# A decoder step with 576 expert gathers: the state space part by groups of four tokens, block 0 finished before the other blocks' projections and attention

## The reference, cut to what matters

```
[q | k | v | u] = x @ w_in + b_in                    # four parts of 512 columns
att = mixture of dilated causal windows over q, k, v  # 8 heads of 64
ssm = S5 state space over u: 32 groups of 16 channels, 64 complex states each
      h[t] = a * h[t-1] + B u[t];  y[t] = Re(C h[t]) + D u[t];  then gelu, a GLU
h   = LN1(ALPHA * x + concat(rms(att), rms(ssm)) @ w_out + b_out)
y   = LN2(ALPHA * h + PEER(h) + sigmoid(h @ w_ple_gate) * (p @ w_ple))
# PEER: 8 heads; h @ w_pq gives queries (4 parts of 512 columns), matched with 128 + 128
# keys; the 16 best of their pairs name experts, each a row of w_down and a row of w_up:
#     sum over experts of  weight * gelu(h . down[e]) * up[e]
```

## Time and profile before

| what | value |
|---|---|
| median of 3 runs | 1949.74 us (1948.12 to 1951.41) |
| profiled execution: its own time, its span | 1951.28 us, 1949.5 us |
| mean granted clock of TensorE | 0.741 of full |
| busy share: PE, DVE, ACT, POOL | 68%, 69%, 41%, 40% |
| moved by the DMA engines | 723.17 MB, of which the gathers 604.02 MB |
| chain that ended last: DMA, PE, DVE, ACT, issue | 37%, 22%, 13%, 7%, 6% |

### The profile page before, as it was taken

The page is one execution under the profiler, slowest core; times in us unless marked ns, Lnnn a source line. Parts: engine busy times, 40 slices in busy tenths (PEclk is TensorE's granted clock), DMA queues, the critical chain, the costliest instruction groups (busy, mean ns, idle before and its releaser), DMA issues.

```text
span 1949.5 us, 23865 instructions
## 1 busy us (share of the span) xinstructions
PE 1326.9 (68%) x7204; PEld 646.9 (33%) x7204; DVE 1350.4 (69%) x3212; ACT 793.6 (41%) x2757; POOL 777.9 (40%) x796
## 2 busy tenths in 40 slices
PE   7999886774764866656664655555746666677876
PEld 6765572331232333324321222122221333322221
DVE  6967898864748779888987753444444467886665
ACT  2132247772424344544543443333333223354554
POOL 0953324443434444455443333233233344444442
PEclk9999996776886677777776677766767555576977
DMA  7012689999999999999999999999999999999997
GB/s 299 1 44 93 200 312 421 397 373 421 411 387 415 352 421 421 421 421 420 417 391 416 421 414 420 420 421 421 422 412 422 421 420 405 412 416 417 413 422 287
DMA packets 101024, 723.17 MB, mean 371 GB/s; under 512 B 12016, under 2 KB 12784, under 8 KB 20784
## 3 DMA queue, kind: packets, MB, share of 16 engines
q0 software_dynamic: 82944, 604.02, 75.5%
q1 hardware_dynamic: 17968, 117.77, 15.4%
HBM read 714.78 MB, written 4.87 MB: 369 GB/s over the span
## 4 chain that ended last, share of the span: by engine, by line
DMA 37%; PE 22%; DVE 13%; ACT 7%; issue 6%; POOL 1%; POOLq 0%; ACTq 0%; DVEq 0%; another core or an unknown queue 0%
DMA R<-d_uv,W 37%; PE bank L1408 8%; DVE R L2169 7%; PE bank L1321 3%; PE bank L1295 3%; PE bank L1162 3%; ACT W L1682 1%; ACT L1679 1%; PE bank L1291 1%; PE bank L1154 1%; ACT W L1687 1%; PE bank L1355 1%; POOL R L919 1%; PE bank L1208 1%; ACT W L1650 1%
## 5 line engine op out<-in xcount | busy, mean ns | idle before, releaser
L919 POOL DMA_INDIRECT R<-d_uv,W x576 | 671.8, 1166 | 1011.1 <-PE bank L1408 832.0
L2169 DVE CUSTOM_DVE_ANT_0 R<-R,W 128x1024 f32<-128x1024 f32 x576 | 696.7, 1223 | 473.1 <-DMA R<-d_uv,W 456.1
L1408 PE MATMUL bank<-R,W 128*32 128x512 f32 x2296 | 473.4, 848 | 558.9 <-ACT W L1687 550.5
L1650 ACT CAST W<-W 128x2 uint32<-128x2 f32 x292 | 55.7, 192 | 883.5 <-DVE W L2169 866.8
L1408 PEld LDWEIGHTS bank<-R,W 128*32 128x32 f32 x2296 | 81.6, 125 | 798.5 <-ACT W L1687 724.6
L1687 ACT ACTIVATE W<-W 128x32 f32<-128x32 f32 x576 | 153.5, 313 | 9.7
L1682 ACT ACTIVATE W<-W 128x1 f32<-128x1 f32 x576 | 138.2, 287 | 9.7
L1321 PEld LDWEIGHTS bank<-E 128*128 128x128 f32 x864 | 123.7, 230 | 35.7 <-issue 35.7
L1321 PE MATMUL bank<-E 128*128 128x128 f32 (+1 forms) x864 | 129.7, 317 | 0.5 <-issue 0.5
L963 PE MATMUL bank<-E,W 128*128 128x256 f32 (+1 forms) x384 | 102.9, 427 | 10.1 <-DMA E<-d_xT 7.9
L963 PEld LDWEIGHTS bank<-E,W 128*128 128x128 f32 x384 | 75.4, 200 | 31.5 <-issue 10.1
(11 more groups left out here) (334 smaller groups left out, 1807.9 us busy)
## 6 DMA issues: line engine op xcount, KB each, us to landing
E<-d_kc SPq DMA_DIRECT2D x8, 2560.0 KB
E<-d_w_pq SPq DMA_DIRECT2D x6, 2048.0 KB, 12.7
E<-d_vc SPq DMA_DIRECT2D x8, 1536.0 KB, 26.2
R<-d_uv,W POOLq DMA_INDIRECT x576
E<-d_w_out SPq DMA_DIRECT2D x4, 2048.0 KB, 12.7
E<-d_vc SPq DMA_DIRECT2D x8, 1024.0 KB, 30.5
W<-d_w_in SPq DMA_DIRECT2D x3, 2048.0 KB, 21.1
W<-d_w_pq SPq DMA_DIRECT2D x3, 2048.0 KB, 8.2
```

The lines of the kernel that those rows point to most:

```text
L919: pool.indirect_dma_start(ring[r], None, A["uv"], bass.IndirectOffsetOnAxis(ap=stage[:, half, s:s + 1], axis=0),).then_inc(landed[r], 16)
L1408: last = mm(acc(half, TG * column_group(js[s], half), TG), wsel[:, r, :], ring[r][:, D + half * 512:D + half * 512 + 512], start=False, st ...
L1650: return nc.scalar.copy(stage[:, half, PAIR * x:PAIR * x + PAIR], egall[:, 0, at])
L2169: last = nc.vector.tensor_tensor_reduce(ring[r][:, 0:D], ring[r][:, 0:D], hrep[:, js[s], :], 1.0, 0.0, ALU.mult, ALU.add, dots[:, x, s:s + 1])
```

## The change

**State space part.** The 512 tokens are taken as 128 chunks of four (`SUB`, `CHUNKS`), and x is laid out with the tokens of a block ordered by their place in the chunk. Inside a chunk the convolution is done by one matrix of 128 x 128 for each group of 32 channels (`T`), which is made on the chip; between chunks runs the scan, with the fourth power of the decay. So one scan holds the whole prompt: `scan` is run 4 times and not 16, POOL carries nothing between blocks, and it runs the sample's recurrence behind the fourth scan.

- `piece_u`: u for 128 channels is 128 products of 32 columns that write 32 rows each, by place in the chunk, into one bank of 512; four such pieces and one for the sample (`us`).
- `turn_b`: 32 transposes that lay out B times the powers of the decay, made by DVE (L1333 to L1346 of the changed kernel); `make_c` (DVE): C times the powers, 31 operations; `kernel_of`, four times 48 products with 4 copies each: the matrix `T`.
- `ssm_in` four times, 8 products over all 128 rows; `ssm_out` four times, 12 products; `z_turn` four times, 16 products and a copy, which put the tokens in order for the GLU after gelu.

**Order.** Ahead of block 0's attention come only the halves of k and q that hold blocks 0 and 1 (x = 0) and v of block 0. q's other halves stand between the heads. k's other halves come behind the first match, and the part of `w_in` that they need is loaded a second time (`w_again`, 2 MB). v of blocks 2, 3 and 4 comes at pairs 0 to 2, the GLU of blocks 1 to 3 at pairs 1 to 7, and of block 0's asks the second behind the first pick, the third at pair 8, the fourth at pair 14. POOL is given four slots after the first projection, two after k's last piece and two after the second ask. The attention of blocks 1 to 3 begins at pair 4 with the spacing as before, `PROJECT_AT` is 38, and picks 1, 2 and 3 are at pairs 1 to 10, 17 to 26 and 25 to 38. The bias table of the attention is loaded in three parts, for block 0 (`pbias_first`), for block 1 (`pbias_second`) and whole.

```diff
...
+    order += [("free", 1), ("ask", 0, 1, 0), ("ask", 0, 1, 1), ("free", 2), ("ask_out", 0, 1), ("match", 0, 1), ("match_out", 0, 1)]
...
-ATT_AT = 1
-GLU_AT = 7
-PROJECT_AT = 35
+ATT_AT = 4
+PROJECT_AT = 38
...
+    for b, glu in ((1, 1), (2, 3), (3, 5)):
+        at[glu].append(("glu_block", b))
+        at[glu + 1].append(("gate_block", b))
+        at[glu + 2].append(("product_rest", b))
+        at[8].append(("sums_rest", b))
...
+    for b, t in ((2, 0), (3, 1), (4, 2)):
+        at[t].append(("piece", number("v", b, 0)))
...
+    look_rest(8, 2)
+    look_rest(14, 3)
...
-    pick(1, 0, 0, 0, 0, 0, 1, 2, 3, 4, 5)
-    pick(2, *range(6, 22, 2), 22, 23)
-    pick(3, *range(24, 40, 2), 40, 41)
+    pick(1, 1, 2, 3, 4, 5, 6, 7, 8, 9, 10)
+    pick(2, *range(17, 27))
+    pick(3, 25, 27, 29, 31, 32, 33, 34, 35, 37, 38)
...
+                for j in range(4):
+                    for k in range(DC):
+                        for step in range(SUB):
+                            o = bank[32 * step:32 * step + 32, c, j * P:j * P + P].rearrange("p (a b) -> p a b", a=QB)
+                            last = mm(o, w_u(c)[:, k, 32 * j:32 * j + 32], xT_by_step[:, :, k, step, :],
+                                      start=(k == 0), stop=(k == DC - 1), skip_group_check=True)
...
+            def kernel_of(q):
...
+                for j in range(4):
+                    for x in range(2):
+                        for step in range(SUB):
+                            r = slice(32 * step, 32 * step + 32)
+                            mm(bank[r, 4, j * P:j * P + 32 * (SUB - step)], Bs[:, 4 * q + j, x, :],
+                               C[:, 4 * q + j, x, 0:SUB - step, :].rearrange("p a b -> p (a b)"),
+                               start=(x == 0), stop=False, skip_group_check=True)
...
+            def free(n):
+
+                if n == 0:
+                    pe.wait_ge(out_full, 1)
+                    pe.wait_ge(at_squared, 1)
+                elif n == 1:
+                    pe.wait_ge(proj_full, number("k", CT - 1, 1) + 1)
+                else:
+                    pe.wait_ge(pq_full, 2)
+                pe.sem_inc(slot_free, HALF if n == 0 else PAIR)
...
```

More of the change, by code:

```diff
@@ L52 @@
 FIRST_BANKS = 1024
-WIDE = [2 * P, 2 * P + ST]
+SUB = 4
+CHUNKS = SEQ // SUB
 ROUND = 1.5 * 2.0 ** 23
@@ L135, with number, piece_bank @@
+def number(kind, c, x):
+    return PIECES.index((kind, c, x))
+def piece_bank(n):
+    kind, c, x = PIECES[n]
+    if kind in ("k", "q") and x == 0 or kind == "u":
+        return c
+    if kind == "us":
+        return 4
+    if kind == "v" and c < 2:
+        return 3
+    return 6 + n % 2
 UNITS = [(qb, h) for qb in range(QB) for h in range(NH)]
 def order_of_front():
-    steps = 4 * QB
-    pieces = {n: [2 * CT + 2 * n, 2 * CT + 2 * n + 1] for n in range(9)}
-    pieces.update({n: [2 * CT + 9 + n] for n in range(9, 12)})
@@ L210, in order_of_front, with unit, turned, piece @@
-    order += [("ask", 0, 3, 0), ("ask", 0, 3, 1), ("free", 2, 3),
-              ("ask_out", 0, 3), ("match", 0, 2), ("match_out", 0, 2), ("match", 0, 3), ("match_out", 0, 3)]
+    def unit(k, *whats):
+        return [(what, i) for what in whats for i in (2 * k, 2 * k + 1)]
+    def turned(k):
+        return unit(k, "turn_probs", "invert") + [("copy_pt", 2 * k + 1)]
+    def piece(kind, c, x):
+        n = number(kind, c, x)
+        return [("piece", n), ("put_v" if kind == "v" else "put", n)]
@@ new lines, in order_of_front @@
+    order = [x for c in range(3) for x in piece("u", c, 0)] + [("turn_b", g) for g in range(8)]
+    order += [("tm", 0), ("ssm_in", 0)] + piece("us", 0, 0) + [("s_in",)] + piece("u", 3, 0)
+    order += [("scan", 0), ("ssm_in", 1), ("tm", 1), ("make_c",)]
+    order += [x for c in range(3) for x in piece("k", c, 0)]
+    order += [("kernel_of", 0), ("ssm_out", 0), ("scan", 1), ("ssm_in", 2), ("tm", 2), ("kernel_of", 1)] + piece("k", 3, 0)
+    order += [("gelu", 0), ("ssm_out", 1), ("kernel_of", 2), ("kernel_of", 3), ("scan", 2), ("ssm_in", 3), ("tm", 3)]
@@ new lines, in order_of_front @@
+    order += piece("q", 0, 0) + [("z_turn", 0), ("gelu", 1), ("ssm_out", 2)] + piece("q", 1, 0) + [("z_turn", 1), ("gelu", 2)]
+    order += piece("q", 2, 0) + piece("q", 3, 0) + [("z_turn", 2), ("piece", number("v", 0, 0))]
+    order += [("scan", 3), ("put_v", number("v", 0, 0)), ("ssm_out", 3)] + unit(0, "scores", "bias", "exps")
+    order += [("gelu", 3)] + turned(0) + unit(1, "scores", "bias", "exps")
+    order += piece("q", 0, 1) + [("z_turn", 3)] + turned(1) + unit(0, "values") + unit(2, "scores", "bias", "exps")
@@ new lines, in order_of_front @@
+    order += [("project_first", n) for n in (3, 2, 0, 1)] + [("rms_inverse", 0), ("residual", 0), ("root", 0)]
+    order += [("normal", 0, 0), ("normal", 0, 1), ("turn", 0), ("turn_out", 0), ("ask", 0, 0, 0), ("ask", 0, 0, 1)]
+    order += [("ask_out", 0, 0), ("match", 0, 0), ("match_out", 0, 0), ("s_ssm_out",), ("free", 0)]
+    order += [("tops", 0, 0, j) for j in range(4)] + piece("k", 0, 1) + piece("k", 1, 1)
+    order += [("cross", 0, 0, 0), ("cross", 0, 0, 1), ("resolve", 0, 0, 0), ("resolve", 0, 0, 1)] + piece("k", 2, 1)
@@ L725, in _ @@
+            rows(0)
+            sp.wait_ge(at_full, 1)
+            sp.wait_ge(at_squared, 1)
+            load(parts_of[0][0], eight(A["w_pq"][0]), in_pq[0])
             sp.wait_ge(sx_ready, 1)
@@ new lines, in z_turn @@
+            def z_turn(q):
+                pe.wait_ge(y_used, q + 1)
+                if q == 0:
+                    pe.wait_ge(t_ready, CT)
+                else:
+                    pe.wait_ge(z_ready, q)
+                for step in range(SUB):
+                    for j in range(4):
+                        last = mm(bank[32 * j:32 * j + 32, 4, step * P:step * P + P],
+                                  ident[:, 32 * step:32 * step + 32], zt[:, j, :], start=True, stop=True)
+                last.then_inc(z_turned, 1)
@@ L1714, in finish_root @@
                 f(lnrow[:, 2:3], lnrow[:, 1:2], ACT.Sqrt).then_inc(y_root, 1)
-            parts = {"piece": put, "tm": set_tm, "s_in": copy_ssm_in, "exps": exps, "norm_out": norm_out,
+            parts = {"put": put, "z_turn": z_turn, "turn_b": put_b, "kernel_of": put_t, "tm": set_tm, "s_in": copy_ssm_in, "exps": exps, "norm_out": norm_out,
                      "copy_pt": copy_pt, "squares": squares, "att_out": att_out, "gelu": gelu,
```

888 lines of the change are left out of this document (495 added, 393 removed).

## The result

| | before | changed |
|---|---|---|
| median, us | 1950.58 (1948.12 to 1952.72, 4 runs) | 1983.76 (1974.8 to 1989.98, 4 runs) |
| ratio, 95% interval | | 1.0167 (1.0126 to 1.0208) |
| profiled execution's span | 1949.5 | 1973.0 |

What follows compares the result with a forecast made beforehand. PE bounds the front, the DMA engines everything from the first gather on. Span 1949.5 - 17.6 (earlier gather) + 26.9 (moved bytes) = 1958.8, median 1959 us, 0.5% slower; range 1937 to 1976.

Steps and rivals of the forecast that it cites:

- (a): PE's work up to the first projection's end: end at 206.6 us, 14.0 earlier; with (b), first gather 17.6 us earlier.
- the price of 67 ns: Cost of each narrow product of u on PE, giving 8.6 us a piece and 34.6 us for four.
- The price of a stall in the clock: In the front, PE slowed by a lower clock behind a wait: 3.0 us more, taken twice, 6.
- The rival of slow narrow products: u's products in the front cost 0.1 us each, 17 us longer, 1976; chance 0.14, shared with "the cover is gone".
- (b): From the first projection's end to the first gather: 7.1 us to h, then 36.9, gather at 250.6.
- A rule and a row: Front: DVE's scans priced alone, up to 60 us longer beside POOL; attention beside POOL's sample work 10 us by the lock.
- (c): Loads and stores moved behind the first gather: 11.3 MB, adding 26.9 us at 421 GB/s.
- (d): PE's added work between the pairs (v, GLUs, two asks): bounds 0 and 8 us, taken as 0.
- The sign named for (d): PE's wait for the fourth ask's w_pq at pair 14, and DVE's for the bias table, show whether (d) is 0.
- The other sign: If DVE's picks are late for block 0's second expert group, POOL waits for W and not for slots.
- The faster rivals: Moved bytes fill gaps behind the first gather, or the front is much shorter: each 1942 us; together, faster, 0.20.
- the cover is gone: Between the pairs, (d)'s 8 us, plus lower clocks at six waits (12 us): 1979; chance 0.14, shared with slow narrow products.

Runs made afterwards that it cites:

- a_again: The changed kernel measured once more with no edit: 1988.94 us, ratio 1.0197 to the kernel before.
- c_light: a_both with v of blocks 2 to 4 and the third and fourth ask summed over one of eight parts: 1959.55 us, ratio 1.0042 to before.
- c_bytes: c_light with only the still used eighth of w_pq loaded for the two asks, 3.67 MB less: 1958.01 us, ratio 1.0040 to before.
- a_both: Changed kernel with block 2's second residual moved ahead of block 1's transposition, and GLU sums and asks spread over pairs: 1972.30 us, ratio 1.0113 to before.
- a_picks: a_both with DVE's picks 2 and 3 laid wider, at pairs 14 to 26 and 28 to 41: 1977.37 us, ratio 1.0141 to before.

## Why the prediction was wrong, point by point

- **(a) The front, 17.6 us earlier: right, a little small.** It is 22.3. PE, timeline of the changed kernel (answers to the earlier trace rows): the pieces of u, `turn_b`, and the fourth piece.

```profile
...
10.49 8.60 PE L971 MATMUL bank<-E,W 128*32 128x128 f32 x223 [10.49 <-DMA E<-d_xT]
...
33.16 8.39 PE L971 MATMUL bank<-E,W 128*32 128x128 f32 x289 [2.77 <-issue]
41.49 3.90 PE L1035 MATMUL bank<-ident,E 128*128 128x128 f32 x32
...
61.02 9.80 PE L971 MATMUL bank<-E,W 128*32 128x128 f32 x256 [2.05 <-ACT W L1687]
...
```

u's first three pieces end at 41.5, 31.0 us for 25.8; with the fourth's 9.8 it is 6.2 us more than 34.6. The first three hold 6.7 us of waits for nothing visible (1.13, 2.77 and 2.77); without them they take 8.1 us each. The fourth stands behind a wait of 2.05 us, in a window with a granted clock of 0.68. So the price of 67 ns held, and what the sum lacked were these waits. `turn_b` takes 3.9, not 7.3, since a transposition is cheaper than the product whose price it got; `kernel_of` 2.2 each, 8.8 for 12.9. The price of a stall in the clock, 3 us twice, came in part: the windows of 10 us from 40 to 60 and 70 to 100 us are granted 0.98 to 1.00, only that from 60 is at 0.68 and that from 100 at 0.83. So not every longer wait costs it. The projection's end, 6.2 us early, is a sum of errors of both signs: 6.2 us too little for u against 3.4 and 4.1 too much for the next two, and more. The rival of slow narrow products is out.

- **(b) 7.1 us to h: right** (7.2; PE's last product of the projection ends at 200.4, and it waits 7.24 for DVE). From h, at 207.6, to the gather 38.3 for 36.9.

```profile
...
196.80 3.60 PE L1245 MATMUL bank<-R,E 128*128 128x512 f32 x8
207.64 1.97 PE L1378 MATMUL bank<-ident,E 128*128 128x128 f32 x8 [7.24 <-DVE E L2351]
...
```

- **A rule and a row.** DVE's 128 x 512 operations in the scans took 0.69 us, as priced. The 10 us that I had worked out from the lock in the Trainium skill, SBUF — State Buffer, section SBUF: two separate sides, did not come: POOL's sample work runs from 126 to 174.5, and PE waits for ACT and not for DVE among the heads. The prediction told the rule one-sidedly, too: on that page it is the operation that starts first that keeps the pair, VectorE's or GpSimd's.
- **(c) 11.3 MB, 26.9 us: the bytes right (11.4), their price an upper bound.** 9.0 us for 5.24 MB in the kernel before, 8.0 for 3.67 with PE's moved work and DVE's picks out, 0.4 with the picks in.
- **(d) "I take 0": the step that failed.** The bounds were 0 and 8, and it was 0 by choice, "since the added loads slow the pairs anyway". The runs put in its place: PE's moved products 13.8 us, of which v 4.3 and the asks 8.6; their heaping at pair 8, 6.4; and the transposition ahead of its residual, 10.7, which the forecast had not seen at all. Together 13.8 + 16.4 = 30.2 us of the 38.4 by which a_again is longer. What is left, c_light's +8.2 us, lies near the 9.3 of the sum without (d). That it is so near is partly luck: the front was 4.7 us better than forecast, and with it and 27.1 us for the bytes that sum is 4.8.
- The sign named for (d), PE's wait for the fourth ask's w_pq, is in the trace: 6.44 us (8.39 in a_again), and DVE waits 2.73 us for the bias table. The DMA engines are full meanwhile. The wait shrinks only together with the bytes (8.66 in c_light, 3.98 in c_bytes), so its own price is open. The other sign is absent: behind the first gather POOL waits for W only once for longer than 0.3 us, 6.11 at pair 29, and not at pair 16.
- The faster rivals are out: neither did the gaps take the bytes nor did the first gather reach 237.4. The slower one, "the cover is gone", is what happened, at nearly four times its 8 us. PE's frees were late, as it said, but not by the difference of two sums. I compared PE's work of pairs 0 to 5 with the transfers' time, 45 to 42, and took it as even. That left out pairs 6 to 14, the heap at pair 8, and a wait that crosses pairs. The last two can be read from the order ahead of a run: two steps of 5.3 and 9.2 us in one pair, and a step at t + 7 that waits for one at t + 11.
- **Still open:** why two profiles of the changed kernel are equal to pair 12, part by 8.8 us up to pair 24 and end 15.7 us apart. Runs of one kernel lie as far apart (1974.8 to 1992.4, and 1941.4 to 1957.9 of the kernel before over all its runs). That the order in which loads and gathers land decides it is only argued. Open too is the stretch from 400 to 460 us, at 320 GB/s in a_both and 387 in the kernel before; a_picks raised it to 346, and the kernel got no shorter.
